# Two of four scatter sums moved between the gate and the up products of each expert pair

## The reference

```python
def moe_ffn(...):
    scores = sigmoid(xf @ w_router)              # 64 experts, 8 groups of 8
    top_idx, gates = best 8 of the 4 best groups # per token; gates normed, times 2.5
    for each expert e, for its tokens:           # nothing is dropped
        y = (silu(x @ w_gate[e]) * (x @ w_up[e])) @ w_down[e]    # 1024 -> 256 -> 1024
    routed[token] += gate * y                    # segment_sum over the 8 choices
    shared = (silu(xf @ ws_gate) * (xf @ ws_up)) @ ws_down
    return routed + shared
h = layer_norm(alpha * h + moe_ffn(h))
```

## Time and profile before

| | us |
|---|---|
| time, median of 3 runs | 1343.06 (1342.52 to 1345.43) |
| the profiled execution's own time | 1344.49 |
| its span in the trace | 1342.5 |
| TensorE busy in the span | 1307.4 (97%) |
| VectorE, ScalarE, GpSimd busy | 423.6, 226.0, 460.3 |
| mean DMA rate over the span | 355 GB/s |

### The profile page before, as it was taken

The page is one execution under the profiler, slowest core; times in us unless marked ns, Lnnn a source line. Parts: engine busy times, 40 slices in busy tenths (PEclk is TensorE's granted clock), DMA queues, the critical chain, the costliest instruction groups (busy, mean ns, idle before and its releaser), DMA issues.

```text
span 1342.5 us, 20094 instructions
## 1 busy us (share of the span) xinstructions
PE 1307.4 (97%) x7754; PEld 696.1 (52%) x7754; DVE 423.6 (32%) x1155; ACT 226.0 (17%) x557; POOL 460.3 (34%) x487
## 2 busy tenths in 40 slices
PE   8999999999999999999989999899999999999997
PEld 5756445545545545444448555454545545545543
DVE  0544462232232222222144443532222222222223
ACT  1254120111110110100122641111011011011011
POOL 2042356444434434332100323443323323323301
PEclk9999999999999999999989999899999999999999
DMA  9862479999999999999985335799999999999994
GB/s 334 341 251 95 148 250 419 420 419 423 421 421 423 423 422 423 424 421 424 406 305 187 126 126 193 268 410 416 424 423 423 423 424 425 424 423 425 424 425 186
DMA packets 98470, 476.24 MB, mean 355 GB/s; under 512 B 20236, under 2 KB 27624, under 8 KB 49120
## 3 DMA queue, kind: packets, MB, share of 16 engines
q1 hardware_dynamic: 75296, 442.32, 80.4%
q0 software_dynamic: 23104, 33.00, 7.0%
HBM read 483.39 MB, written 24.32 MB: 378 GB/s over the span
## 4 chain that ended last, share of the span: by engine, by line
PE 76%; SPq 10%; DMA 7%; DVE 3%; POOL 1%; issue 1%; ACT 1%; POOLq 0%; DVEq 0%; ACTq 0%
PE bank L739 26%; PE bank L766 13%; PE bank L701 13%; SPq L529 10%; PE bank L820 7%; DMA ring<-in_w_up_dram 5%; PE bank L831 5%; PE bank L1086 3%; PE bank L1131 1%; PE bank L755 1%; DMA arena<-h_rows,rank_i 1%; PE bank L823 1%; PE bank L668 1%; PE bank L951 1%; PE bank L986 1%
## 5 line engine op out<-in xcount | busy, mean ns | idle before, releaser
L739 PE MATMUL bank<-ring,arena 128*64 128x256 f32 x2784 | 315.5, 383 | 11.6 <-DMA ring<-in_w_up_dram 6.6
L2109 POOL DMA_INDIRECT arena<-h_rows,rank_i x256 | 257.1, 1004 | 93.6 <-issue 80.7
L739 PEld LDWEIGHTS bank<-ring,arena 128*64 128x64 f32 x2784 | 203.0, 139 | 133.8 <-issue 32.7
L701 PE MATMUL bank<-arena 128*128 128x512 f32 x512 | 247.1, 606 | 0.0
L1800 DVE TENSOR_TENSOR arena<-arena,bank 128x256 f32<-128x256 f32 x64 | 26.9, 421 | 574.5 <-ACT arena L1322 574.5
L2115 POOL DMA_INDIRECT arena<-g_rows,rank_i x64 | 63.7, 995 | 382.5 <-DVE arena L1796 363.1
L766 PE MATMUL bank<-ring,arena 128*64 128x512 f32 x704 | 160.8, 599 | 0.0
L1329 ACT ACTIVATE arena<-bank 128x512 f32<-128x512 f32 x128 | 76.4, 597 | 413.2 <-PE bank L766 413.2
L1750 DVE STREAM_TRANSPOSE arena<-arena 128x256 f32<-128x256 f32 x256 | 141.4, 609 | 13.3 <-DMA arena<-h_rows,rank_i 7.1
L739 PE MATMUL bank<-arena 128*64 128x256 f32 x1280 | 143.5, 379 | 1.9 <-DMA arena<-in_w_up_dram 1.9
L701 PEld LDWEIGHTS bank<-arena 128*128 128x128 f32 x512 | 87.7, 191 | 87.7 <-issue 86.7
(11 more groups left out here) (254 smaller groups left out, 894.8 us busy)
## 6 DMA issues: line engine op xcount, KB each, us to landing
ring<-in_w_up_dram SPq DMA_DIRECT2D x44, 2048.0 KB, 26.0
ring<-in_w_down_dram SPq DMA_DIRECT2D x44, 2048.0 KB, 23.8
ring<-in_w_gate_dram SPq DMA_DIRECT2D x43, 2048.0 KB, 24.2
arena<-in_w_gate_dram SPq DMA_DIRECT2D x20, 2048.0 KB, 24.8
arena<-in_w_up_dram SPq DMA_DIRECT2D x20, 2048.0 KB, 25.9
arena<-in_w_down_dram SPq DMA_DIRECT2D x20, 2048.0 KB, 23.9
ring<-in_w_in_dram SPq DMA_DIRECT2D x8, 2048.0 KB, 20.7
ring<-in_w_o_dram SPq DMA_DIRECT2D x4, 2048.0 KB, 13.8
```

The costliest lines, as they stand in the source:

```text
L701: return mm(bank[SUM_BANKS[n][half]][0:w, :], selg[:, u, t0:t0 + w], y_sb[:, u, half * 512:(half + 1) * 512], start=False, stop=stop, skip ...
L739: last = mm(bank[5][64 * e:64 * e + 64, part * F:(part + 1) * F], xgT[:, u, kk, 64 * e:64 * e + 64], w[e][:, kk, :], start=(kk == 0), stop ...
L2109: pool.indirect_dma_start(out=xg[:, q % 2, b, :], out_offset=None, in_=h_rows, in_offset=bass.IndirectOffsetOnAxis(ap=rank_i[:, at:at + 1] ...
```

## The change

In each pair but the opening one, the two sums of the pair in front that go to chunk 1 are issued between the gate products and the up products. The waits for `y_ready` and `selg_ready`, which they need, move with them. The third sum stays behind the up products, the fourth behind the transposes. The number of instructions stays the same.

```diff
@@ -731,6 +731,11 @@
                         pe.wait_ge(h_ready[l], r * 32 + p)
                     for part in range(2):
                         if part == 1:
+                            if not opens:
+                                pe.wait_ge(y_ready[l], r * 64 + p * 2)
+                                pe.wait_ge(selg_ready[l], r * 32 + p)
+                                scatter(l, 1 - u, 1, 0)
+                                scatter(l, 1 - u, 1, 1)
                             weights = arrived(1)
                         w = weights if isinstance(weights, list) else [weights[:, e, :] for e in range(2)]
                         w = [x.rearrange("p (k f) -> p k f", k=KC) for x in w]
@@ -742,10 +747,6 @@
                         last.then_inc((gates_used[l], gu_done[l])[part], 1)
 
                     if not opens:
-                        pe.wait_ge(y_ready[l], r * 64 + p * 2)
-                        pe.wait_ge(selg_ready[l], r * 32 + p)
-                        scatter(l, 1 - u, 1, 0)
-                        scatter(l, 1 - u, 1, 1)
                         scatter(l, 1 - u, 2, 0)
                     elif shared_piece:
                         for piece in range(3):
```

## The result

| | before | after |
|---|---|---|
| median, us | 1343.37 (1342.52 to 1345.43) | 1398.93 (1398.52 to 1400.52) |
| profiled execution, us | 1344.49 | 1399.23 |
| its span | 1342.5 | 1397.2 |
| ratio of the times | | 1.0406, 95% interval 1.0388 to 1.0424 |

The change makes the kernel 55.6 us slower. The prediction was 1400 us, with a range of 1379 to 1419. The sums stay on L701.

A forecast was written before the change was run, and what follows sets the result against it. TensorE was taken to become the bound of both stages: 1.12 us a pair over 31 pairs, less slack, adds 26.3 us in layer 0 and 30.6 in layer 1, 56.9 us on 1343.06, so 1400 us, range 1379 to 1419.

The forecast's parts named there:

- the slack summed over a layer: TensorE's own 14.35 us a pair over 31 pairs lies below DMA's pace by 8.41 us in layer 0, 4.10 in layer 1.
- The price of a pair: Each pair on TensorE costs 1.93 - 0.81 = 1.12 us more, 15.47 in place of 14.35.
- ahead of the up products: Two moved sums between gate and up products add 1.93 us a pair, bounds 1.71 to 2.14.
- the transposes 0.81 us earlier: Behind the up products, transposes stand at 1.87 us in place of 2.68 from the sums' start; saving bounds 0.71 to 0.92.
- rows 7: Opening pair's profile rows: from the second product's end to the first transpose 0.36 us, with 0.31 us of weight load open.
- transposes to down products: The stretch behind the transposes stays at 1.18 us, since the same operations stand there after the change.
- The gap before the transposes: TensorE idles about 0.9 us before the transposes, waiting for the hidden rows, in each pair but the opening ones.
- The moved waits and the later release: y_ready and selg come 2.6 us early; the up slot's release comes 1.9 us later; both costed at nothing.
- Filling the wait for up weights: Rival: the sums take the place of TensorE's 21.5 us of waits for up weights, giving 1323 us; chance 0.02.
- DMA did not stay the bound: Rival: weight arrival keeps bounding the stages, only the part behind the last up weights shortens, giving 1342.9 us; chance 0.03.
- The clock stayed at 1.00: Rival judged: clock falls in the new gaps, up products lose 1.69 us a pair, giving about 1506 us; chance 0.03.
- The weight load of the transposes: Before the first transpose, 0.31 us of load taken as open; hidden by the rule, the sum would be about 19 us lower.

The follow-up runs named there:

- waits_only: Kernel before, with only the waits for y_ready and selg_ready moved ahead of the up products, all sums behind them; 1380.51 us against 1382.48, ratio 0.9971 to 1.0002.
- half_down_after: Changed kernel, each down-slot refill bringing only expert 0's half of the weights; 1423.34 us against 1381.29 for the kernel before, ratio 1.0276 to 1.0318.
- pair30_only: Kernel before, with the two sums moved in pair 30 of layer 1 alone; 1382.19 us against 1381.29, ratio 0.9989 to 1.0013.
- early_ha: Changed kernel, with sigmoid and first product done during the two moved sums; 1385.53 us against 1381.29 for the kernel before, ratio 1.0009 to 1.0037.
- before_again: Kernel before, unedited, measured and traced again in another set; 1364.38 us against 1365.41, ratio 0.9979 to 1.0021.
- fourth_ahead: Changed kernel, with the fourth sum moved from behind the transposes to in front of them; 1413.04 us against 1382.48 for the kernel before, ratio 1.0199 to 1.0245.

## Why the prediction was right

**The bound.** Right. That DMA was busy throughout said nothing about an edit on TensorE; the slack summed over a layer did. The changed kernel waits for no weights, DMA ends early, and halving the down traffic changes next to nothing. By the first pair of traces: 62 x 1.07 = 66.3 us, less 12.5 us of slack, is 53.8; measured were 53.9 us in the two stages and 54.7 us in the span. One part of the slack was something else than the prediction took it for: of layer 1's 4.10 us, 1.69 us are not a wait for weights but the up products at a lower clock behind it. The sum holds all the same, since the changed kernel has neither the wait nor the slow products.

**The price of a pair.** 1.12 us predicted, 1.07 measured, and the terms differ more than the sum:

- ahead of the up products 1.93 us predicted, 1.92 measured;
- gate and up products 7.00 us before and 3.55 + 3.60 = 7.15 after (385.27 to 388.82 and 375.32 to 378.92). I had left out these 0.15 us;
- the transposes 0.81 us earlier predicted, 1.11 measured (1.57 us behind the start of the sums in place of 2.68). The transposes are recorded 0.06 us behind the second product, where rows 7 had let me expect 0.36;
- transposes to down products 1.18 us predicted, 1.30 measured: the two transposes take 0.51 us together where they took 0.39, and the fourth sum follows them. That their loads are no longer hidden is my explanation of it.

1.92 + 0.15 - 1.11 + 0.12 = 1.08. So the forecast of 1400 us for 1399 is closer than its terms deserve: the saving was put 0.30 us too small and two terms of 0.15 and 0.12 us were left out, and these nearly cancel. With only one of the two mended the forecast would have been about 1381 or 1417 us, still slower and within the range, so the direction and the mechanism don't hang on this luck. The gap before the transposes was predicted as 0.9 us. Counting from the end of the one sum (378.92 + 0.11 + 0.86 = 379.89) to 380.49 it is 0.6; the row lists 0.44, from the modelled end of the last record.

**The moved waits and the later release** cost nothing, as said. `waits_only` shows the first. For the second speak the last up weights of layer 0, which land as early as before, and `half_down_after`, in which less DMA work leaves the pair at 15.42 us.

**The rivals.** Filling the wait for up weights brought nothing in the one pair where it was tried (`pair30_only`). DMA did not stay the bound. The clock stayed at 1.00 in spite of a gap in every pair. The busy time by stretch of the changed kernel, one row for each layer (length, engines, clock, DMA share, GB/s):

```profile
212.00:660.00 448.00, 435.20 (x2615) 205.46 (x2616) 111.26 (x239) 45.78 (x87) 177.96 (x178) 1.00 1.01 422
...
902.00:1370.00 468.00, 454.70 (x2729) 214.29 (x2730) 114.87 (x246) 48.56 (x92) 145.78 (x147) 1.00 0.97 402
```

**The weight load of the transposes.** By the rule of the Trainium skill ("TensorE: Matmul & The Clock Gate", part 2, step by step) the load would have been hidden, and a pair 0.31 us cheaper than I had it. In time the trace lies nearer to that than to my term: the transposes are recorded 0.06 us behind the hidden rows, and 0.12 us were lost later. But it doesn't show a load pulled ahead: the load is recorded at 380.49 us, with its transpose and behind the hidden rows.

## What to carry to other kernels

Work that TensorE does while it waits for another engine is free only where it is. Before such work is moved, compare what stays there with the length of the chain that it covers: here 1.82 us with two sums was enough for 1.57 us, and 0.97 us with one was not. If work must go, bring a part of the chain with it, as `early_ha` does, which won back 0.72 of the 1.07 us. Where TensorE and DMA are both nearly full, sum the slack between them over the whole stage, and don't read it off a few waits near its end: 0.13 us a pair was all that layer 1 had.

## What was unexpected of the hardware

- The same kernel took 1343 to 1345, 1365 and 1381 to 1382 us in different sets, at granted clocks of 0.984 to 0.993, and chip number 6 gave both 1382.48 and 1344.83 us. What makes a set slow stays open. Undisturbed pairs kept their pace to 0.01 us, so the difference lies in single places: the first pair behind the opening one took 20.8 us (238.72 - 217.96 in `before_again`) where it took 14.35, and signals were late.
- In the slower sets the signal of the last up product reached ScalarE late in layer 0 when sums of chunk 1 stood behind it: the sigmoid started mostly 0.5 to 2.2 us behind the up products there, and up to 6.7 us in the first pairs, against 0.12 us in the fast sets and in most steady pairs of layer 1. It depended on what stood behind the product: about 2 us with both sums of chunk 1, 0.85 us with one of them, 0.12 us in most pairs where only sums of chunk 2 did, even two of them (`fourth_ahead`). The last gate product in `early_ha` also has both sums of chunk 1 behind it, and its signal was on time in layer 0 (0.12 us). In the records the late signal came together with the landing of a store of the learned tokens' rows (420.64 and 420.66 us in one pair of `waits_only`). Whether that is the cause stays open: the runs without stores fell into a set that has no late signals, and steady pairs of layer 1, which has no stores, show up to 0.56 us in `waits_only`.
- The 32 stores, off the path within the pairs, cost 8.8 us by the medians and 6.6 us by the traces.
